# One matmul on nine partitions for the distance biases, and the squares of x split between two engines, at the start of a decoder layer

## What is computed

```python
mod = silu(c) @ w_ada + b_ada                      # 9 x 2048 numbers
sh1, sc1, g1, sh2, sc2, g2, sh3, sc3, g3 = split(mod, 9)
h = rms_norm(x, norm_ffn1) * (1 + sc1) + sh1       # needs the mean of x*x of each token
x = x + 0.5 * g1 * (silu(h @ w1_gate) * (h @ w1_up)) @ w1_down
...
s_w = q @ k * scale + rel_bias[t5_bucket(dist)]    # NSA logits: a bias by distance for each of 8 heads
```

## Time and profile before

| | |
|---|---|
| median of 3 runs | 2060.33 us (2058.78 to 2060.92) |
| profiled execution, its own time | 2060.54 us |
| its span | 2058.7 us |
| TensorE busy | 2024.6 us, 98% of the span |
| VectorE, ScalarE, GpSimd busy | 1398.9, 873.7, 36.6 us |
| moved by DMA | 533.10 MB, 259 GB/s over the span |

### The profile page before, as it was taken

The page is one execution under the profiler, slowest core; times in us unless marked ns, Lnnn a source line. Parts: engine busy times, 40 slices in busy tenths (PEclk is TensorE's granted clock), DMA queues, the critical chain, the costliest instruction groups (busy, mean ns, idle before and its releaser), DMA issues.

```text
span 2058.7 us, 26899 instructions
## 1 busy us (share of the span) xinstructions
PE 2024.6 (98%) x9331; PEld 1605.0 (78%) x9331; DVE 1398.9 (68%) x1864; ACT 873.7 (42%) x1119; POOL 36.6 (2%) x56
## 2 busy tenths in 40 slices
PE   7999999999999999999999999999999999999998
PEld 4668888788888888787787888788888888888886
DVE  4557887877778889896556669777775545545454
ACT  3344434344443434543444644544444444434333
POOL 0000000000000000000005000000000000000000
PEclk9999999999999999999999999999999999999999
DMA  8998999799989889698967138589986777675654
GB/s 309 387 349 301 332 318 322 261 292 297 278 303 327 308 319 347 221 365 290 290 194 260 42 134 305 165 276 291 295 251 197 197 199 205 198 217 197 199 186 133
DMA packets 343366, 533.10 MB, mean 259 GB/s; under 512 B 80874, under 2 KB 99397, under 8 KB 342377
## 3 DMA queue, kind: packets, MB, share of 16 engines
q1 hardware_dynamic: 342648, 529.90, 77.6%
q10 hardware_dynamic: 624, 1.97, 0.3%
HBM read 520.04 MB, written 3.89 MB: 254 GB/s over the span
## 4 chain that ended last, share of the span: by engine, by line
PE 93%; DVE 2%; issue 1%; DMA 1%; ACT 1%; SPq 0%; ACTq 0%
PE ps L825 29%; PE ps L827 29%; PE ps L826 29%; PE ps L869 1%; PE ps L906 1%; DMA ada_half<-in_w_ada_dram 1%; PE ps L854 1%; DVE ada_acc L1941 1%; DVE w_lo L1923 1%; PE ps L1372 1%; PE ps L1375 1%; PE ps L1402 1%; PE ps L1207 0%; ACT w_hi L1496 0%; DMA raw<-in_w_uq_dram 0%
## 5 line engine op out<-in xcount | busy, mean ns | idle before, releaser
L1496 ACT ACTIVATE w_hi<-raw 128x1024 fp32r<-128x1024 f32 (+1 forms) x657 | 688.9, 1054 | 929.0 <-PE ps L827 552.6
L1923 DVE TENSOR_TENSOR w_lo<-raw,w_hi 128x1024 fp32r<-128x1024 f32 (+1 forms) x657 | 796.0, 1220 | 408.0 <-ACT w_hi L1496 402.4
L825 PE MATMUL ps<-w_hi,hT_hi 128*128 128x512 f32 (+1 forms) x1856 | 741.7, 400 | 6.5 <-DVE hT_lo L2058 4.3
L827 PE MATMUL ps<-w_hi,hT_lo 128*128 128x512 f32 (+1 forms) x1856 | 731.8, 394 | 0.0
L826 PE MATMUL ps<-w_lo,hT_hi 128*128 128x512 f32 (+1 forms) x1856 | 731.7, 394 | 0.0
L825 PEld LDWEIGHTS ps<-w_hi,hT_hi 128*128 128x128 f32 x1856 | 349.8, 188 | 102.4 <-issue 15.3
L827 PEld LDWEIGHTS ps<-w_hi,hT_lo 128*128 128x128 f32 x1856 | 349.8, 188 | 83.6
L826 PEld LDWEIGHTS ps<-w_lo,hT_hi 128*128 128x128 f32 x1856 | 350.1, 189 | 79.8 <-issue 0.5
L1941 DVE SCALAR_TENSOR_TENSOR ada_acc<-ada_raw,silu_c,ada_acc 128x512 f32<-128x512 f32 x420 | 315.4, 751 | 8.1
L825 PE MATMUL ps<-w_hi,actT_hi 128*128 128x512 f32 x704 | 280.0, 398 | 0.0
L827 PE MATMUL ps<-w_hi,actT_lo 128*128 128x512 f32 x704 | 279.1, 396 | 0.0
(11 more groups left out here) (245 smaller groups left out, 947.3 us busy)
## 6 DMA issues: line engine op xcount, KB each, us to landing
ada_raw<-in_w_ada_dram SPq DMA_DIRECT2D x224, 512.0 KB, 5.5
raw<-in_w_gate_dram SPq DMA_DIRECT2D x176, 512.0 KB, 4.9
raw<-in_w_up_dram SPq DMA_DIRECT2D x176, 512.0 KB, 4.9
raw<-in_w_down_dram SPq DMA_DIRECT2D x176, 512.0 KB, 5.0
raw<-in_w_in_dram SPq DMA_DIRECT2D x72, 512.0 KB, 5.8
ada_half<-in_w_ada_dram SPq DMA_DIRECT2D x14, 2048.0 KB, 12.9
raw<-in_w_out_dram SPq DMA_DIRECT2D x32, 512.0 KB, 5.4
actT_lo<-norm_tmp SPq DMA_DIRECT2D x240, 32.0 KB, 3.2
```

What stands on the lines that cost most here:

```text
L825: pe.matmul(bank, lhs_hi, rhs_hi, start=start, stop=False)
L827: return pe.matmul(bank, lhs_lo, rhs_hi, start=False, stop=stop)
L1496: act.activation(part(U, w_hi, s), part(U, raw, s), ACT.Copy).then_inc(hi_done, 1)
L1923: dve.tensor_tensor(part(U, w_lo, s), part(U, raw, s), part(U, w_hi, s).bitcast(F32), ALU.subtract)\
```

## The change

- **Biases.** `rel_rep` and the copy on GpSimd go. One matmul with `rel_sb` itself (33 by 9) as the left operand yields nine rows of 384, one for each column, on nine partitions. VectorE copies them once (9 x 384). The store now reads each of the nine rows 128 times (`unsqueeze(1).broadcast_to`) and writes the same bytes to the same places.
- **Place.** The matmul stands behind the first round of turning x (`turn_norm("ffn1", 0)`) and the copy behind `first_low(0)`, both formerly ahead of everything.
- **Squares.** ScalarE squares the first tile of x, VectorE the second, with four instructions that multiply and sum (`second_squares`). `x_rstd` waits for four squares of ScalarE in place of eight; VectorE's own lie ahead of it in order.
- **Tables.** A Silu of one column stands ahead of the squares on ScalarE.

```diff
@@ sync, gpsimd @@
-            pool.wait_ge(rel_landed, 16 * 2)
-            pool.wait_ge(rel_set, 2)
-            pool.tensor_copy(rel_rep[:, :, :], rel_sb[:, :].unsqueeze(2).broadcast_to([BUCKETS + 1, HEADS + 1, P]))\
-                .then_inc(rows_set, 1)
@@ tensor @@
-                if i == 2:
-                    pe.wait_ge(rev_done, HEADS + 1)
...
-            pe.wait_ge(rows_set, 4)
-            bias_rows(0, HEADS + 1)
             start_part(0, 0)
...
             turn_norm("ffn1", 0, x_tile)
+            bias_rows()
             start_part(1, 0)
...
+            def bias_rows():
+
+                pe.wait_ge(rel_set, 2)
+                pe.wait_ge(rel_landed, 16 * 2)
+                pe.matmul(ps[0:HEADS + 1, 3, 0:384], rel_sb[:, :], bucket_sb[:, :], start=True, stop=True)\
+                    .then_inc(rev_mm, 1)
@@ scalar @@
-            first_squares(0)
+            act.wait_ge(rows_set, 3)
+            act.activation(stat[:, 5, 3:4], ones[:, 0:1], ACT.Silu)
+            first_squares()
...
             load_root_table()
-            first_squares(1)
             root("ffn1", TT)
...
-            act.wait_ge(rev_done, HEADS + 1)
-            dma(bias_scratch.ap(), rev_b[:, :, :]).then_inc(rev_stored, 16)
+            act.wait_ge(rev_done, 1)
+            dma(bias_scratch.ap().rearrange("p h n -> h p n"), rev_b[:, :].unsqueeze(1).broadcast_to([HEADS + 1, P, 384]))\
+                .then_inc(rev_stored, 16)
@@ vector @@
+            def second_squares():
+
+                dve.wait_ge(x_landed[1], 16)
+                for c in range(D // CW):
+                    xs = x_sb[:, 1, c * CW:(c + 1) * CW]
+                    then_wait(dve.tensor_tensor_reduce(act_sg[:, c % 2, :], xs, xs, 1.0, 0.0, ALU.mult, ALU.add,
+                                                       x_sq[:, 1, c:c + 1]))
...
-            copy_bias_rows()
+            second_squares()
             norm_x("ffn1")
...
             first_low(0)
+            copy_bias_rows()
             start_lo(0, 1)
```

More of the change, by code:

```diff
@@ L349, in decoder_layer @@
             v_rows = sb("v_rows", [NV, P], within=s)
-            rel_rep = sb("rel_rep", [BUCKETS + 1, HEADS + 1, P], within=s)
+            behind_rel = sb("behind_rel", [P, (HEADS + 1) * P], within=s)
             silu_pad = sb("silu_pad", [P, KD, 32], within=s)
@@ L353, in decoder_layer @@
             behind_half = sb("behind_half", [P, 2240], within=s)
-            rev_b = sb("rev_b", [P, HEADS + 1, 384], within=s)
+            rev_b = sb("rev_b", [HEADS + 1, 384], within=s)
+            behind_rev = sb("behind_rev", [P, HEADS * 384], within=s)
             unshifted = sb("unshifted", [P, 2 * TT, CW], within=s)
@@ L513, in blocked_before @@
             return u + FF // CW - 1 - BLOCKS_FROM if f == 1 else u - BLOCKS_FROM
-        def bias_bank(h):
-            return T_BANK + 1 if h == HEADS else h % 4
         def ada_use(q, p):
@@ L1080, in first_panel @@
                 pe.wait_ge(nrm["ffn1"]["T_lo_done"], 2 * i + e // 2 + 1)
-                if j < 2 and u == 0:
-                    pe.wait_ge(rev_done, (6, 8)[j])
-                elif j < 2:
+                if (u, j) == (0, 1):
+                    pe.wait_ge(rev_done, 1)
+                elif u == 1 and j < 2:
                     pe.wait_ge(spilled, 2 * j + 2)
@@ L1644, in _, with first_squares @@
             dma(pe_sb[:, DK:DK + VD], pe_cmp_v[0]).then_inc(pe_landed, 16)
-            def first_squares(t):
-                act.wait_ge(x_landed[t], 16)
+            def first_squares():
+                act.wait_ge(x_landed[0], 16)
                 for c in range(D // CW):
[L1650 to L1654, removed]
-            first_squares(0)
+                    if c >= 2:
+                        act.wait_ge(nrm["ffn1"]["squares"], c - 1)
+                    act.activation(norm_tmp[:, c % 2, :], x_sb[:, 0, c * CW:(c + 1) * CW], ACT.Square,
+                                   accum_out=x_sq[:, 0, c:c + 1]).then_inc(nrm["ffn1"]["squares"], 1)
+            act.wait_ge(rows_set, 3)
+            act.activation(stat[:, 5, 3:4], ones[:, 0:1], ACT.Silu)
+            first_squares()
             act.wait_ge(v_done, 1)
@@ L1714, in down_unit @@
                         x_squares(("mix", "final")[f], res[U.stage]["x_added"], before(U))
-            act.wait_ge(rows_set, 3)
             load_root_table()
-            first_squares(1)
             root("ffn1", TT)
@@ L1977, in rstd @@
                 then_wait(dve.tensor_tensor(out_, r, e, ALU.mult))
+            def second_squares():
[4 more added lines that the diff above has]
+                                                       x_sq[:, 1, c:c + 1]))
             def x_rstd(n):
-                dve.wait_ge(nrm[n]["squares"], 2 * (D // CW))
+                dve.wait_ge(nrm[n]["squares"], D // CW)
                 then_wait(dve.tensor_reduce(stat[:, 0, 0:TT], x_sq[:, :, :], AX.X, ALU.add))
@@ L2177, in copy_bias_rows @@
             def copy_bias_rows():
[L2179 to L2182, removed]
+                dve.wait_ge(rev_mm, 1)
+                dve.tensor_scalar(rev_b[:, :], ps[0:HEADS + 1, 3, 0:384], 1.0 / SCALE, None, ALU.mult).then_inc(rev_done, 1)
             def add_part(i):
```

## The result

The changed kernel takes 2068.0 us (2067.5 to 2070.6), the kernel before 2060.3 us (2058.8 to 2061.3): a ratio of 1.0041 (95% interval 1.0028 to 1.0054). The forecast of 2053.0 us and its range were wrong, and so was the sign. Of the two halves of the forecast the start came close to what was described. The store did not: the first rival is what happened.

The account below looks back on a forecast made before the run. TensorE, busy 98% of the span, was the bound, with TensorE's order and the transfers bounding the start; 8.2 us less a 0.6 us wait left 7.6, so 2060.54 - 7.6 = 2052.9, stated as 2053.0 us, range 2051.0 to 2060.0.

Parts of the forecast that it names:

- the first rival: Store from nine rows drains slowly and clogs the weight loads queued on the same engines: 2060 to 2075 us; chance 0.22.
- The squares: At the start, VectorE's four squares take 681 ns plus 83 to read the sum each, 3.2 us in all, to 13.3.
- the spread of rstd: At the start, the spreading of rstd comes at 15.5 us, 9.9 us earlier than before.
- the bias matmul: At the start, one matmul in place of nine costs 1.3 us on TensorE's path behind the turning of x.
- The queue no longer ran dry: In SP's load queue, panel 6's load is issued earlier, closing the transfer hole and saving 6.9 us.
- half 2: At the start, the chain to `start_half` 2 comes 8.6 us earlier, at 32.6; TensorE is done with it at 34.4.
- half 3: At the start, it still lands at 37.2; TensorE waits 2.8 us for it and has multiplied it at 40.7.
- Half 5: At the end of the start, it lands at 55.2 and is multiplied by 57.4 in place of 65.60, 8.2 us earlier.
- the sum: 8.2 us won by half 5, less a 0.6 us wait at chunk 2's `add_start`, leaves 7.6 us.
- the term of the store: The bias store from nine partitions takes 8.2 us, one row per engine, and costs TensorE no wait.
- The upper bound: For the bias store: all nine rows at one engine's rate, 24.1 GB/s, would take 73 us.
- The cover: Behind the store, the first panel's `w_lo` leads TensorE by 7.6 us, which a store of 8 us cannot use up.

Follow-up runs that it names:

- the spread store: The changed kernel with the store's rows laid two or twelve partitions apart, or each made on eight partitions: 2053.6 to 2054.2 us.
- tail_far: step12 with one more store of the same size and form at the end, from partitions 0, 12, ... 96: 2063.7 us.
- bias_near: The changed kernel without the squares split (all squares on ScalarE as before), store still from nine neighbouring partitions: 2068.5 us.
- step12: The changed kernel with the nine rows on partitions 0, 12, ... 96, by a twelvefold copy of `rel_sb` on GpSimd: 2054.1 us.
- wide8: The changed kernel with each row made on eight partitions (0 to 71) and each copy stored sixteen times: 2054.2 us, again 2053.6 us.
- step2: The changed kernel with the nine rows on partitions 0, 2, ... 16: 2053.7 us.
- the run four apart: step12 with one more store of the same size and form at the end, from partitions 0, 4, ... 32: 2071.3 us.
- squares_only: The kernel before with only the squares split and the table load moved; wide bias matmuls, copies and store kept: 2060.6 us.

## Why the prediction was wrong, point by point

**The start was right in the main.** The squares took 0.69 and 0.08 us each (forecast 0.68 and 0.08), the spread of rstd came at 15.36 (15.5), the bias matmul cost 0.8 us (1.3). The queue no longer ran dry. TensorE waited 5.0 us in two pieces rather than 2.8 in one: it was ready for half 2 at 30.1 and not at 32.6, waited 3.19 us for it, which was not foreseen, multiplied it in 3.64 us rather than 1.8, and then waited 1.79 us for half 3, which landed at about 38.7 and not at 37.2. Half 5 was done at 58.8 (57.4). The gain at the store's issue was 7.24 us, against 7.6 in the sum, and with the spread store it shows in the time: 6.6 to 7.8 us.

**The step that failed is the term of the store**: "If nine engines carry one row each, 8.2 us; I take that, since it is nearest to the only store of this size." The nearest row was a store of the same size but of another shape, from 128 partitions. Nine engines with a row each do take about 8 us, as tail_far shows (1.77 MB at 226 GB/s are 7.8 us). But the rows must lie in nine groups. On nine neighbours the fullest group holds four rows, and the store takes 33.6 us alone and 34 beside the loads. The upper bound took 24.1 GB/s, an engine's share of 386, for all nine rows and so gave 73 us; that it lies near the rate of a group is luck, and the right count was four rows, 32 us. The prediction weighed the row of the old store against the port map of the Trainium skill ("SBUF — State Buffer", section "Door 1: The DMA port swizzle") and took the row. The map was right in its mechanism, and the estimate of 28.5 us from its 27.6 GB/s was too short, since the rate was 24 to 25. The slow store should have been the likeliest case: no row of the trace contradicted it.

**Rival 1 had the mechanism.** With half of the engines' time left to the loads, T of 34 us and the lead of 7.6, its own formula gives waits of 34/2 - 7.6 = 9.4 us; 8.5 were measured. That they lie so near is in part luck: the lead was misread (next paragraph), the loads moved at a quarter of their rate and not at half (3.22 MB in 32 us, 101 GB/s of 386), and in bias_near, with the same store, TensorE's two waits for `w_lo` were 5.95 and 5.60 us. What the formula left out is what follows a wait: near half the clock behind each, another 5 to 6 us, so 14.5 in all where it allowed 7 at T = 30. Its range of 2060 to 2075 holds the result; the prediction gave it a chance of 0.22.

**The cover was misread.** The prediction took the `w_lo` that ends at 250.75 and TensorE's start at 258.34 for one panel, the first behind the store. Counted off, twelve matmuls to a panel, that `w_lo` belongs to the panel that TensorE begins at 255.53, and its load went out at 240.44, ahead of the store. The first load behind the store in the kernel before, its landing (us from the issue), and TensorE's start on its panel:

```profile
248.19 0.37 SPq L561 DMA_DIRECT2D raw<-in_w_gate_dram  x1
...
raw<-in_w_gate_dram SPq DMA_DIRECT2D x1, 512.0 KB, 8.7
...
264.75 0.48 PE L825 MATMUL ps<-w_hi,hT_hi 128*128 128x512 f32 x1
```

In the changed kernel, where TensorE waits for this panel, it begins 2.4 us after the landing (260.0 to 262.36). So before the change the load could have taken an estimated 14.2 us from its issue without a wait. In step12, wide8 and step2 it took 6.3, 6.2 and 4.9 us and the next one 7.5, 10.8 and 10.8, beside drains of 12 to 16 us: no wait. In the changed kernel it took 19.3, beside a drain of 34.

**What stays open.** Shown are that the partitions decide the store's speed, and at which rate. That the loads are held because their pieces queue behind the store's on the same engines is argued from the queues (0.184 us for a piece of the store in place of 0.068, while a load's piece is hardly slower); no run gave the store engines of its own.

## What to carry to other kernels

Price a store that reads few partitions by the fullest group of partitions that share a way out, not by its size: 24 to 25 GB/s a group here, with four neighbours in one and, by the run four apart read with the map above, 0 and 32 too. If few rows are to be spread over memory, make them on many partitions first (here a copy of 0.24 us on GpSimd and the same single matmul) or lay them apart; here two apart was enough. And price a wait of TensorE with the slow microseconds that can follow it: behind the 8.5 us of waits they cost an estimated 5.4 us more.

## What the runs showed of the hardware

Behind the slow store SP took 3.6 to 4.5 us for an issue in place of 0.37, though the store stood on another queue. Long issues are not the store's alone: at the start of the same kernel, with no store in flight and the loads at some 385 GB/s, the issues at 14.25 and 22.86 took 3.60 and 5.92 us.

In squares_only one VectorE square lasted twice as long as the others while GpSimd copied `rel_rep` (1.45 us there, 1.14 without the squares beside it). VectorE's and then GpSimd's timeline:

```profile
11.21 1.50 DVE L1983 CUSTOM_DVE_ANT_0 silu_gate<-x_sb 128x512 f32<-128x512 f32 x1
...
12.75 0.69 DVE L1983 CUSTOM_DVE_ANT_0 silu_gate<-x_sb 128x512 f32<-128x512 f32 x1
...
24.61 0.15 DVE L1988 TENSOR_REDUCE stat<-x_sq 128x2 f32<-128x8 f32 x1
```

```profile
10.71 1.45 POOL L763 COPY rel_rep<-rel_sb 33x1152 f32<-33x1152 f32 x1 [8.41 <-DMA bucket_sb<-bucket_one_hot]
```

The two overlap from 11.21 to 12.16; that one held up the other is read from this overlap and was not tried by itself. The sum of the squares came at 24.61, not at the expected 23.2, since this copy began 1.1 us later than before and took 0.3 longer, and the nine matmuls followed it.
